# Sample scores on strips of 32 rows in a YOCO-style decoder step

## The reference

```python
s_past = (jnp.einsum('bqhc,bkc->bhqk', q_lat, c_past)      # q_lat: 16 heads x 256 latent
          + jnp.einsum('bqhr,bkr->bhqk', q_rope, kr_past)) # q_rope: 16 heads x 64 rotary
s = jnp.concatenate([s_past, s_new], axis=-1) * ATTN_SCALE
p = jax.nn.softmax(s, axis=-1)
o = jnp.einsum('bhqk,bkc->bqhc', p[..., :P], c_past) + ...   # the same latents are the values
```

## Time and profile before

| | us |
|---|---|
| median of three runs | 735.84 |
| span of the profiled execution | 733.3 |
| median of the runs less that span | 2.5 |
| TensorE busy in the span | 724.7 |
| VectorE, ScalarE, GpSimd busy | 308.4, 410.0, 534.7 |

### The profile page before, as it was taken

How to read it: one execution, slowest core, us unless ns; L and a number is a source line. 1 busy time by engine, 2 the same in 40 slices (tenths; PEclk the granted TensorE clock), 3 DMA queues, 4 the chain that set the end, 5 groups by cost and what they waited for, 6 DMA issues and landing times.

```text
span 733.3 us, 16703 instructions
## 1 busy us (share of the span) xinstructions
PE 724.7 (99%) x6255; PEld 709.0 (97%) x6255; DVE 308.4 (42%) x781; ACT 410.0 (56%) x747; POOL 534.7 (73%) x252
## 2 busy tenths in 40 slices
PE   9999999999999999999999999999999999999996
PEld 9999999999999999999999888799999999999995
DVE  5446986233333222232588766753233332321002
ACT  7877555455444444555677576564564444444542
POOL 5895778869878888888868122149878888888891
PEclk9999999999999999999999999999999999999999
DMA  7864455656777755666565898326546555555641
GB/s 261 272 201 138 132 166 177 201 173 222 237 235 232 241 179 175 199 202 201 175 255 193 274 373 315 133 66 218 178 148 200 181 188 177 192 175 190 204 153 60
DMA packets 44842, 144.68 MB, mean 197 GB/s; under 512 B 5650, under 2 KB 6674, under 8 KB 44530
## 3 DMA queue, kind: packets, MB, share of 16 engines
q1 hardware_dynamic: 44498, 143.50, 59.0%
q0 software_dynamic: 144, 0.40, 0.1%
q10 hardware_dynamic: 144, 0.02, 0.0%
HBM read 142.42 MB, written 1.48 MB: 196 GB/s over the span
## 4 chain that ended last, share of the span: by engine, by line
PE 95%; DVE 2%; ACT 1%; DMA 1%; issue 0%; SPq 0%; DVEq 0%; ACTq 0%
PE ps L1400 29%; PE ps L1401 29%; PE ps L1402 29%; PE ps L1808 1%; PE ps L1784 1%; PE ps L1728 1%; DMA h<-xT 1%; PE ps L1537 1%; PE ps L1655 0%; PE ps L1446 0%; PE ps L1788 0%; PE ps L1714 0%; ACT whi L485 0%; DVE ps L867 0%; PE ps L1716 0%
## 5 line engine op out<-in xcount | busy, mean ns | idle before, releaser
L419 POOL TENSOR_TENSOR wlo<-raw,whi 128x1024 fp32r<-128x1024 f32 x221 | 527.0, 2406 | 181.5 <-ACT whi L485 181.4
L1400 PE MATMUL ps<-xhi,whi 128*128 128x264 f32 x1000 | 286.2, 286 | 0.0
L1401 PE MATMUL ps<-xlo,whi 128*128 128x264 f32 x1000 | 283.4, 283 | 0.0
L1402 PE MATMUL ps<-xhi,wlo 128*128 128x264 f32 x1000 | 283.2, 283 | 0.0
L485 ACT ACTIVATE whi<-raw 128x1024 fp32r<-128x1024 f32 x221 | 232.7, 1054 | 50.7 <-PE ps L1402 48.6
L1401 PEld LDWEIGHTS ps<-xlo,whi 128*128 128x128 f32 x1000 | 188.5, 188 | 0.1
L1400 PEld LDWEIGHTS ps<-xhi,whi 128*128 128x128 f32 x1000 | 188.3, 188 | 0.3
L1402 PEld LDWEIGHTS ps<-xhi,wlo 128*128 128x128 f32 x1000 | 187.6, 188 | 0.0
L1400 PE MATMUL ps<-ahi,whi 128*128 128x264 f32 x352 | 100.0, 284 | 0.0
L1402 PE MATMUL ps<-ahi,wlo 128*128 128x264 f32 x352 | 99.9, 284 | 0.0
L1401 PE MATMUL ps<-alo,whi 128*128 128x264 f32 x352 | 99.9, 284 | 0.0
(11 more groups left out here) (272 smaller groups left out, 1152.6 us busy)
## 6 DMA issues: line engine op xcount, KB each, us to landing
raw<-w_stream SPq DMA_DIRECT2D x221, 512.0 KB, 3.3
pg<-pages SPq DMA_DIRECT2D x64, 288.0 KB, 4.3
pg<-w_ukT SPq DMA_DIRECT2D x1, 2048.0 KB, 9.4
pg<-w_uv SPq DMA_DIRECT2D x1, 2048.0 KB, 10.2
h<-xT SPq DMA_DIRECT2D x4, 264.0 KB, 4.5
raw<-w_stream SPq DMA_DIRECT2D x4, 256.0 KB, 4.6
y_out<-raw SPq DMA_DIRECT2D x4, 198.0 KB, 2.0
wsraw<-wsT SPq DMA_DIRECT2D x1, 512.0 KB, 5.2
```

Source lines behind the costliest of these rows:

```text
L419: pool.tensor_tensor(wlo[:, c % RING, :], raw[:, c % RING, :], whi[:, c % RING, :].bitcast(F32), ALU.subtract).then_inc(lo_ready, 1)
L1400: pe.matmul(out, whi_, mhi, start=start, stop=False)
L1401: pe.matmul(out, whi_, mlo, start=False, stop=False)
L1402: return pe.matmul(out, wlo_, mhi, start=False, stop=stop)
```

## The change

A page's keys and values become two tensors in memory and two DMAs: keys (latent and rotary, 1280 bytes a row) on 128 partitions, values on 64 partitions with two keys' rows of 1024 bytes beside each other; two pages share the 128 partitions. A strip now has 32 rows, 16 heads for the first 64 keys of its pages and 16 heads for the last 64, and 128 columns. The queries are padded with zeros: qsl holds 16 zero columns on either side of the 16 heads, so that a window of 32 columns puts the heads in the lower or the upper half; qsr is block-diagonal over the two key halves. The maximum needs both halves of a strip: a reduce, a shuffle that exchanges the 16-row halves, and a minimum. One square is turned, not two. total_hi and total_lo move into a gap of memory.

```diff
+            total_hi = sb("total_hi", [P, T], F32R, g)
+            total_lo = sb("total_lo", [P, T], F32R, g)
...
-        pg = sb("pg", [P, BUFS, PAGES, PAGE])
-        qsl = sb("qsl", [P, KL, NS, H])
-        qsr = sb("qsr", [P, 2, NS, H])
+        pg = sb("pg", [P, BUFS, PAGES * PAGE])
+        qsl = sb("qsl", [P, KL, NS, 3 * H])
+        qsr = sb("qsr", [P, NS, 2, H])
+        page_keys = pg[:, :, 0:PAGES * KEYT].rearrange("p b (g k) -> p b g k", g=PAGES)
+        page_vals = pg[:, :, PAGES * KEYT:PAGES * PAGE].rearrange("p b (j z c) -> p b j z c", j=PAGES // 2, z=2)
+        nmx = sb("nmx", [P, 2])
+        TURN16 = [(i + H) % (2 * H) for i in range(2 * H)]
...
-                sp.dma_start(pg[:, s % BUFS, g, :], pages[at]).then_inc(pages_ready[s % BUFS], 16)
+                b, rows = s % BUFS, slice(HALF * (g % 2), HALF * (g % 2) + HALF)
+                sp.dma_start(page_keys[:, b, g, :], pages[at]).then_inc(pages_ready[b], 16)
+                sp.dma_start(page_vals[rows, b, g // 2].rearrange("p z c -> p (z c)"), page_values[at]).then_inc(
+                    pages_ready[b], 16)
...
-                act.activation(ps_, ps[:, 5, 0:2 * P], ACT.Exp, bias=nms[:, s:s + 1],
+                act.activation(ps_, ps[:, 5, 0:P], ACT.Exp, bias=nms[:, s:s + 1],
...
-                act.activation(pT, key_views(6)[:, :, 0:P], ACT.Copy).then_inc(ptc_done, 1)
+                act.activation(pT, ps[:, 6, 0:P], ACT.Copy).then_inc(ptc_done, 1)
...
-                    dve.memset(qsr[ROPE:P, 0], 0.0).then_inc(qsr_done, 1)
-                    dve.memset(qsr[0:ROPE, 1], 0.0).then_inc(qsr_done, 1)
+                    dve.memset(qsr[:], 0.0).then_inc(qsr_done, 1)
+                    dve.memset(qsl[:], 0.0).then_inc(qsr_done, 1)
...
-                dve.tensor_reduce(nms[:, s:s + 1], ps[:, 5, 0:2 * P], AX, ALU.max, negate=True).then_inc(snm_done, 1)
+                dve.tensor_reduce(nmx[:, 0:1], ps[:, 5, 0:P], AX, ALU.max, negate=True).then_inc(snx_done, 1)
+                dve.wait_ge(snx_done, 2 * s + 1)
+                dve.stream_shuffle(nmx[:, 1:2], nmx[:, 0:1], TURN16).then_inc(snx_done, 1)
+                dve.wait_ge(snx_done, 2 * s + 2)
+                dve.tensor_tensor(nms[:, s:s + 1], nmx[:, 0:1], nmx[:, 1:2], ALU.min).then_inc(snm_done, 1)
...
-                dve.tensor_tensor(lw, sums, ww[:, 0:4, :], ALU.mult).then_inc(sum_step, 1)
+                dve.tensor_tensor(lw, sums, ww[:, 0:4, :].unsqueeze(2).broadcast_to([NS, 4, 2, H]),
+                                  ALU.mult).then_inc(sum_step, 1)
...
-                    return ps[32 * j:32 * j + H, 5, 0:2 * P].rearrange("p (g k) -> p g k", g=2)
+                    return ps[32 * j:32 * j + 2 * H, 5, 0:P].rearrange("p (g k) -> p g k", g=2)
                 for c in range(KL):
-                    for j in range(4):
-                        pe.matmul(strip(j), qsl[:, c, s, :], pg[:, b, 2 * j:2 * j + 2, c * P:(c + 1) * P], start=c == 0,
-                                  stop=False)
-                for z in range(2):
-                    for j in range(4):
-                        last = pe.matmul(strip(j)[:, :, z * ROPE:(z + 1) * ROPE], qsr[:, z, s, :],
-                                         pg[:, b, 2 * j:2 * j + 2, LAT:KEYT], start=False, stop=z == 1)
+                    for z in range(2):
+                        queries = qsl[:, c, s, H - z * H:3 * H - z * H]
+                        at = c * P + z * HALF
+                        for j in range(4):
+                            pe.matmul(strip(j), queries, page_keys[:, b, 2 * j:2 * j + 2, at:at + HALF],
+                                      start=c == 0 and z == 0, stop=False)
+                for j in range(4):
+                    last = pe.matmul(strip(j), qsr[:, s].rearrange("p z h -> p (z h)"),
+                                     page_keys[:, b, 2 * j:2 * j + 2, LAT:KEYT], start=False, stop=True)
...
-                for b in range(2):
-                    last = pe.transpose(ps[:, 6, 2 * b * P:(2 * b + 1) * P], ps_[:, b * P:(b + 1) * P], ident[:])
-                last.then_inc(spt_done, 1)
+                pe.transpose(ps[:, 6, 0:P], ps_, ident[:]).then_inc(spt_done, 1)
...
-                for b in range(2):
+                for z in range(2):
                     for j in range(4):
-                        last = pe.matmul(ps[32 * j:32 * j + H, 7, 0:LAT], pT[:, b, 32 * j:32 * j + H],
-                                         pg[:, s % BUFS, 2 * j + b, KEYT:PAGE], start=b == 0, stop=b == 1)
+                        at = (2 * j + z) * H
+                        last = pe.matmul(ps[32 * j:32 * j + H, 7, 0:LAT], pT[:, at:at + H], page_vals[:, s % BUFS, j, z, :],
+                                         start=z == 0, stop=z == 1)
```

More of the change, by code:

```diff
@@ L41 @@
 PAGE = KEYT + LAT
+HALF = P // 2
 BUFS = 3
@@ L56 @@
 X2_AT = 24736
+TOTAL_AT = 24088
 STAGES = {}
@@ L87, in wait, with build @@
         eng.wait_ge(sem, i * k + c if k else c)
-def build(nc, xT, w_stream, w_uv, gains, v_gain, lat_gain, q_gain, wsT, ws00_in, bs, cosT, sinT, w_ukT, pages, table,
+def build(nc, xT, w_stream, w_uv, gains, v_gain, lat_gain, q_gain, wsT, ws00_in, bs, cosT, sinT, w_ukT, pages, page_values, table,
           y_out, c_out, kr_out, v_out):
@@ L161, in build @@
         with ExitStack() as g:
-            x2_gap = sb("x2_gap", [P, X2_AT], c=g)
+            x2_gap = sb("x2_gap", [P, TOTAL_AT], c=g)
+            total_hi = sb("total_hi", [P, T], F32R, g)
+            total_lo = sb("total_lo", [P, T], F32R, g)
+            total_gap = sb("total_gap", [P, X2_AT - TOTAL_AT - 2 * T], c=g)
             x2hi = sb("x2hi", [P, KD, T], F32R, g)
@@ L180, in build @@
         swap = work[:, 6, 0:P]
-        total_hi = sb("total_hi", [P, T], F32R)
-        total_lo = sb("total_lo", [P, T], F32R)
         SPLIT_SUMS = ("ffn0", "mix1", "q", "ffn1")
@@ L201, in build @@
         pr = tt[:].rearrange("p a t -> p (a t)")[:, 0:6 * P].rearrange("p (e k) -> p e k", e=2)
-        ps_ = sq[:].rearrange("p a t -> p (a t)")[:, 0:2 * P]
-        pT = sq[:].rearrange("p a t -> p (a t)")[:, 2 * P:4 * P].rearrange("p (b k) -> p b k", b=2)
+        ps_ = sq[:].rearrange("p a t -> p (a t)")[:, 0:P]
+        pT = sq[:].rearrange("p a t -> p (a t)")[:, 2 * P:3 * P]
         flat = work[:].rearrange("p a t -> p (a t)")
@@ L207, in build @@
         qrs = flat[:, 7 * T:7 * T + PAIRS * NS].rearrange("p (a s) -> p a s", a=PAIRS)
-        last_pages = pg[:, BUFS - 1].rearrange("p g k -> p (g k)")
+        last_pages = pg[:, BUFS - 1]
         ukT = last_pages[:, 0:H * LAT].rearrange("p (h c) -> p h c", h=H)
         uvraw = last_pages[:, 0:H * LAT].rearrange("p (h v) -> p h v", v=P)
-        scratch = pg[:, 0].rearrange("p g k -> p (g k)")
+        scratch = pg[:, 0]
         taken = [0]
@@ L223, in build @@
         dd, ww = by_strip(room(NS, 5 * H)), by_strip(room(NS, 5 * H))
-        lw = room(NS, 4 * H).rearrange("p (j h) -> p j h", j=4)
+        lw = room(NS, 8 * H).rearrange("p (j z h) -> p j z h", j=4, z=2)
         ll, mn, wn = (room(NS, H) for _ in range(3))
@@ L281, in build @@
         pv_done, ohi_done, olo_done = map(sem, ("pv_done", "ohi_done", "olo_done"))
-        ssc_done, snm_done, sexp_done, spt_done, ptc_done, spv_done, os_done = map(
-            sem, ("ssc_done", "snm_done", "sexp_done", "spt_done", "ptc_done", "spv_done", "os_done"))
+        ssc_done, snx_done, snm_done, sexp_done, spt_done, ptc_done, spv_done, os_done = map(
+            sem, ("ssc_done", "snx_done", "snm_done", "sexp_done", "spt_done", "ptc_done", "spv_done", "os_done"))
         new_done, nst_done, nsn_done, cns_done, wz_done, mn_done, dd_done, ww_done, sum_step, wt_done = map(
@@ L805, in _ @@
             act.wait_ge(qlt_done, 1)
-            act.activation(qsl[:, 0].rearrange("p s (g j) -> p s g j", j=4),
+            act.activation(qsl[:, 0, :, H:2 * H].rearrange("p s (g j) -> p s g j", j=4),
                            ps[:, 6, :].rearrange("p (g j s) -> p s g j", g=4, j=4)[:, 0:NS], ACT.Copy).then_inc(qsla_done, 1)
@@ L1243, in _ @@
             dve.wait_ge(qrs_done, PAIRS)
+            dve.wait_ge(qsr_done, 2)
             for z in range(2):
                 for e in range(2):
-                    dve.tensor_copy(qsr[64 * z:64 * z + 64, z].rearrange("p s (a e) -> p a s e", e=2)[:, :, :, e],
+                    dve.tensor_copy(qsr[64 * z:64 * z + 64, :, z].rearrange("p s (a e) -> p a s e", e=2)[:, :, :, e],
                                     qrs[64 * e:64 * e + 64]).then_inc(qsr_done, 1)
@@ L1287, in sample_maximum @@
                 dve.wait_ge(ssc_done, s + 1)
-                dve.tensor_reduce(nms[:, s:s + 1], ps[:, 5, 0:2 * P], AX, ALU.max, negate=True).then_inc(snm_done, 1)
-            maxima, sums = (ps[0:NS, 5, x * P:(x + 1) * P].rearrange("p (j h) -> p j h", j=4)[:, :, 0:H] for x in (1, 2))
+                dve.tensor_reduce(nmx[:, 0:1], ps[:, 5, 0:P], AX, ALU.max, negate=True).then_inc(snx_done, 1)
[3 more added lines that the diff above has]
```

(18 more changed lines are left out.)

2 lines of the change are left out of this document (1 added, 1 removed).

## The result

The changed kernel takes 748.96 us (748.41 to 749.52) where the kernel before takes 735.58 (734.94 to 736.31): the ratio is 1.0183, 95% interval 1.017 to 1.0195. The forecast was 735.0, range 733.5 to 737.6. The span of the profiled execution went from 733.3 to 747.8 us.

What follows compares the result with a forecast made beforehand. TensorE, busy 99% of the 733.3 us span, was taken as the bound. Attention compute -0.93, weights() +0.07 and pages +0.1 gave -0.8 us, so 735.0 us; own range 733.9 to 736.0, with rivals 733.5 to 737.6.

Steps and rivals of the forecast that it cites:

- part 5: Page loads in the attention stage: 16 SP issues a sequence, 0.515 us apart; s6's pages arrive just as wanted, +0.1 us.
- the second rival: SP's page issues decide and the kernel gets slower: gain gone from 0.53 us an issue, 737.9 us at 0.56; chance 0.2.
- All other sequences keep 1 us or more: Page loads: except for s6, pages land at least 1 us before the scores want them, so no other wait.
- Part 1: Scores on TensorE: 40 passes of 128 columns replace 1.30 us a sequence; saving 0.14 us, bounds 0.07 to 0.20.
- the scores' rival: Weight loads of 32 columns set the pace, scores stay at 1.30 us a sequence; -0.2 us, so 735.6; chance 0.06.
- Part 2: Turn of the probabilities on TensorE: one transpose instead of two, saving 0.11 us a sequence; value products unchanged.
- Part 3: Maximum on VectorE: shorter reduce, then shuffle, minimum and perhaps a permutation load (0.08) delay the exponentials by 0.35 us.
- Who pays: Delay against TensorE saving for sample sequences s0 to s7: s0 +0.26, s3 and s4 +0.03 each, other five -0.25 each; -0.93 us.
- part 4: Small things: copy, memsets and moved totals cost nothing; two wider operations in weights() put +0.07 us on the path, once.

Runs made afterwards that it cites:

- after_128: Changed kernel, but a page's values come as 128 rows x 1024 B instead of 64 rows x 2048 B (sum over cached values wrong); 740.81 us, 1.0081.
- one_dma: Changed kernel, but each page comes in one DMA of 128 partitions x 2304 B as in the kernel before (attention over the cache wrong); 733.74 us, 0.9976.
- keys_first: Changed kernel, but from the third sequence on the 8 key DMAs are issued first, then the 8 value DMAs; 744.21 us, 1.0126.
- pool_values: Changed kernel, but the values of the third to eighth sequence are issued by GpSimd and not by SP; 745.75 us, 1.0141.
- half_values: Changed kernel, but only the first 1024 B of each of the 64 value rows are loaded, and both value passes read these; 748.41 us, 1.0173.

## Why the prediction was wrong

The step that failed is in part 5: "Six page issues took 2.91 us, so one starts 0.515 us after the other", used for both DMAs of a page. It was the price of a 128-row DMA, and the values have 64 rows; no row of the kernel before had that shape, so it needed two bounds and got one number. From that step the last DMA of s6 was to be issued at 447.8 us. The runs, by the start of that issue in the traces, and by the time of the whole kernel:
- 451.9 in `after_128`, where 0.515 holds. What the step lacks here are long issues, of 0.7 to 1.6 us, five in these 38 us; the kernel before has four of them too between 414 and 450 (1.1 to 1.3 us), one of them among its 16 issues in 10.72 us, so its trace held the warning. In time this is 7.1 us over `one_dma` (740.81 against 733.74), so two DMAs a page lose even where both have 128 rows.
- 456.3 in `keys_first`, with 0.65 us for a value DMA: 3.4 us more in time.
- 461.5 in the changed kernel, where each key DMA behind a value DMA is dear as well: 4.75 us more in time. Of the 13.7 us between 447.8 and 461.5, 2.4 lie ahead of s3: its first issue comes at 416.75 and not at 414.34, behind the 11.4 us that s2's 16 issues take.

The row of 10.72 us was also read in two ways that it does not bear, as a bound on moving a page and as SP held up by queued transfers: about 1.0 us of it is SP's wait for s1's attend(), which frees the buffer for s4.

So the second rival won: SP's issues decide, and beyond its own point (0.53 to 0.56 us an issue; measured 0.64 without the long ones). Its reason, SP held up by transfers that queue, is what `pool_values` shows, but not the changed kernel's cause: `half_values` moves 22% fewer bytes, its keys land in 2.5 us instead of 3.5, and its issues are no faster. Its price was too small for the same reason as the forecast's, and because it charged one wait, at s6; s3 to s7 all wait, and the longest wait is followed by work at the lower clock. "All other sequences keep 1 us or more" fell with it.

The rest, step by step, by `one_dma`:
- Part 1: the saving is 0.21, just past the upper end of the bounds (0.07 to 0.20) and not the middle. Weight loads of 32 columns took 110 ns (112 estimated) and hid; the scores' rival falls with that.
- Part 2: 0.11, as forecast.
- Part 3: the reduce of 128 columns took 0.28 us (0.285), shuffle and minimum start 0.32 and 0.51 us after the reduce, and the delay is 0.70 - 0.45 = 0.25, not 0.35. Loading the permutation took 14 ns each time and not 80. By the Trainium skill's rule (Vector Engine (DVE) Microarchitecture Reference, 3.8) one load would do; the trace shows the load ahead of every shuffle (x8), and that it hardly matters.
- Who pays: s0 +0.17 (forecast +0.26), s3 and s4 -0.07 and -0.08 (+0.03), s1, s2, s5 and s6 -0.30 to -0.34 (-0.25). Who pays and who gains was right but for the sign at s3 and s4; the sum, with s7's column, is -1.6 instead of -0.86 (-0.93 and the 0.07 of part 4), because part 1's saving was put too low and part 3's delay too high.
- Part 4: s7's column, totals and weights() included, is 0.33 shorter (forecast 0.18): the 0.07 does not show.

The Trainium skill's rule that the time to start a DMA is usually small (DMA: Bandwidth & Descriptors, Issuing engines are not separate DMA queues) was set aside by the forecast, rightly: here SP's issue time, with the waits and the lower clock that follow from it, is all of the loss against `one_dma`. Having set it aside, the forecast still priced it at 0.1 us.

What stays open: why 64 partitions cost more, what the long issues wait for, and why the DMA engines at a share near 1 move 248 and 267 GB/s with two DMAs a page (the changed kernel, `pool_values`) and 393 with one. None of the kernels that compute everything beat the kernel before; the gain of 1.5 us needs one DMA a page, and the one such kernel tried pays it back in the turn.

## What to carry to other kernels

Price a transfer by its issues before its bytes: count them per issuing queue, take start-to-start distances over a long stretch with its outliers in it, and of the shape in question; where the trace has no DMA of that shape, bound it. A layout that suits the engines but splits one DMA in two, or loads half of the partitions, has to win more than the issuing queue loses. Where such a queue falls behind, every later consumer can wait: here five sequences did, and the longest wait was followed by work at half the clock.

## What the runs showed of the hardware that was not expected

- An issue on 64 partitions: 0.47 us and 0.65 from start to start, against 0.33 and 0.515 for 128 rows; with 16 B in a row 16, 32, 48, 96 and 128 rows take 0.38 (the DMA of 128 rows ahead of them 0.33).
- It is not local: the 128-row DMA behind it takes 0.45.
- DMA share says little of the bound: 0.65 and 0.97 in two kernels of nearly the same time, with 10.7 and 12.2 us of waits for pages (`half_values`, after).
- After a wait of 7.0 us the granted clock was 0.50, the 1.2 GHz level: the scores behind it took 1.94 us for 1.08 (s5's and s4's record in the timeline).
